# First attention by pairs of heads in a software pipeline, with value products alternating between column halves

## The reference, cut to what matters

```python
logits = jnp.einsum('bnqhgd,bnshd->bhgnqs', q, k_blk, preferred_element_type=jnp.float32) * (HEAD_DIM ** -0.5)
logits = logits + bias.reshape(N_KV_HEADS, GROUP, 1, BLOCK, 2 * BLOCK)
logits = jnp.where(valid, logits, -jnp.inf)
m = jnp.maximum(logits.max(axis=-1, keepdims=True), sink)
p = jnp.exp(logits - m)
denom = p.sum(axis=-1, keepdims=True) + jnp.exp(sink - m)
probs = (p / denom).astype(v_blk.dtype)
o = jnp.einsum('bhgnqs,bnshd->bnqhgd', probs, v_blk)
return o @ w_o + b_o
```

## Time and profile before

| | |
|---|---|
| median of 3 runs | 1185.15 us (1185.14 to 1188.02) |
| profiled execution, its own time | 1187.22 us |
| its span, first to last instruction | 1185.4 us |
| mean granted TensorE clock | 0.925 |
| TensorE busy | 1071.2 us, 90% of the span |
| first attention | 309.9 to 384.1 us |

### The profile page before, as it was taken

The page is one execution under the profiler, slowest core; times in us unless marked ns, Lnnn a source line. Parts: engine busy times, 40 slices in busy tenths (PEclk is TensorE's granted clock), DMA queues, the critical chain, the costliest instruction groups (busy, mean ns, idle before and its releaser), DMA issues.

```text
span 1185.4 us, 17311 instructions
## 1 busy us (share of the span) xinstructions
PE 1071.2 (90%) x7061; PEld 889.1 (75%) x7062; DVE 521.9 (44%) x944; ACT 404.1 (34%) x682; POOL 152.8 (13%) x216
## 2 busy tenths in 40 slices
PE   3799999989787879999996999879899999999966
PEld 2599999988755869999995999678555646646556
DVE  5545554336632255554336538674232222222254
ACT  3443333433343353334335556633201101101053
POOL 5233331110000123333011000000100000000000
PEclk8799999999766889999998999878899999999988
DMA  6334433436400115453453332048288988988501
GB/s 261 142 107 177 167 143 133 160 122 277 152 1 1 72 71 172 182 190 117 176 216 118 143 112 80 1 170 340 94 356 339 380 336 350 372 339 351 214 1 36
DMA packets 25645, 212.52 MB, mean 179 GB/s; under 512 B 2000, under 2 KB 5344, under 8 KB 5728
## 3 DMA queue, kind: packets, MB, share of 16 engines
q1 hardware_dynamic: 25568, 211.43, 46.2%
HBM read 210.35 MB, written 1.07 MB: 178 GB/s over the span
## 4 chain that ended last, share of the span: by engine, by line
PE 81%; DVE 6%; ACT 5%; issue 3%; POOL 3%; DMA 0%; POOLq 0%; DVEq 0%; ACTq 0%
PE ps L1107 45%; PE ps L1443 9%; PE ps L1428 5%; PE ps L1457 5%; PE ps L1465 4%; PE ps L1098 3%; DVE mix L1564 2%; DVE wl L613 2%; ACT wh L606 2%; POOL sq L479 1%; ACT work L752 1%; PE ps L1201 1%; PE ps L1200 1%; PE ps L1413 1%; PE ps L1144 1%
## 5 line engine op out<-in xcount | busy, mean ns | idle before, releaser
L613 DVE TENSOR_TENSOR wl<-ring,wh 128x2048 fp32r<-128x2048 f32 (+2 forms) x110 | 223.3, 2034 | 225.3 <-ACT wh L606 225.3
L606 ACT ACTIVATE wh<-ring 128x2048 fp32r<-128x2048 f32 (+2 forms) x110 | 187.1, 1705 | 318.6 <-PE ps L1107 314.1
L1107 PE MATMUL ps<-xh,wh 128*128 128x256 f32 (+3 forms) x760 | 218.9, 288 | 8.9 <-DVE xl L2074 7.0
L1107 PE MATMUL ps<-xh,wl 128*128 128x256 f32 (+3 forms) x760 | 216.6, 285 | 0.0
L1107 PE MATMUL ps<-xl,wh 128*128 128x256 f32 (+3 forms) x760 | 216.4, 285 | 0.0
L1107 PEld LDWEIGHTS ps<-xh,wh 128*128 128x128 f32 (+3 forms) x760 | 143.2, 188 | 10.9 <-issue 9.2
L1107 PEld LDWEIGHTS ps<-xh,wl 128*128 128x128 f32 (+3 forms) x760 | 143.2, 188 | 0.2
L1107 PEld LDWEIGHTS ps<-xl,wh 128*128 128x128 f32 (+3 forms) x760 | 143.1, 188 | 0.0
L1443 PE MATMUL ps<-wring,xb 128*64 128x512 f32 x512 | 112.7, 592 | 2.3 <-issue 2.3
L1107 PE MATMUL ps<-acth,wh 128*128 128x272 f32 (+1 forms) x352 | 102.6, 292 | 3.8 <-POOL actl L494 3.8
L1107 PE MATMUL ps<-acth,wl 128*128 128x272 f32 (+1 forms) x352 | 101.4, 288 | 0.0
(11 more groups left out here) (334 smaller groups left out, 1618.5 us busy)
## 6 DMA issues: line engine op xcount, KB each, us to landing
wring<-in_w_eg SPq DMA_DIRECT2D x32, 2048.0 KB, 10.4
ring<-in_w_gu SPq DMA_DIRECT2D x22, 2048.0 KB, 7.9
wring<-in_w_ed SPq DMA_DIRECT2D x16, 2048.0 KB, 8.3
ring<-in_w_dn SPq DMA_DIRECT2D x16, 1408.0 KB, 5.9
ring<-in_w_z SPq DMA_DIRECT2D x7, 2048.0 KB, 7.8
ring<-in_w_out SPq DMA_DIRECT2D x4, 1152.0 KB, 5.1
ring<-in_w_q SPq DMA_DIRECT2D x2, 2048.0 KB, 14.0
ring<-in_w_o SPq DMA_DIRECT2D x2, 2048.0 KB, 10.5
```

The costliest lines, as they stand in the source:

```text
L606: act.activation(wh[:, j, 0:size], ring[:, slot, j * size:(j + 1) * size], ACT.Copy)\
L613: dve.tensor_tensor(wl[:, j, 0:size], ring[:, slot, j * size:(j + 1) * size], wh[:, j, 0:size].bitcast(F32), ALU.subtract).then_inc(sem("l ...
L1107: ins = mm(o, p, q, start=first and n == 0, stop=last and n == 2)
```

## The change

The unit is now a pair of heads u = 0 to 7 (`HEAD_PAIRS`). Its four tiles t are ordered by block first: both heads' block 0, then both heads' block 1, one PSUM bank each. TensorE runs scores(u + 2), turn(u), outputs(u - 1); DVE runs shares(u), logits(u + 2), attended_low(u - 2); ACT runs exps(u + 1), turned(u), attended_high(u - 1). Maximum, exponentials and scalings are for four tiles at a time, so the small operations come eight times. `outputs(u)` makes each of the four steps for head 2u and then head 2u + 1, so that successive products go to the left and right column half. The last transpose turns keys 0 to 127 of block 0 in place of the 16 meta keys alone, so that ACT copies a head's 512 columns in one instruction. `pT` has four buffers. The low part of w_o's second half moves from before the first logits to after logits(1). The removed loops are those printed above; the diff shows the new code.

```diff
-        pT = [mix[:, 2 * i:2 * i + 2, :].rearrange("p a b -> p (a b)")[:, 0:4 * P] for i in range(2)]
+        pT = [mix[:, 2 * i:2 * i + 2, :].rearrange("p a b -> p (a b)")[:, 0:4 * P] for i in range(4)]
...
+        HEAD_PAIRS = NH // 2
+        def keys_of(t):
+            return (0, N_META + P) if t < 2 else (N_META, 2 * P)
+        def weights_of(u, t):
+            return lg[u % 4 // 2][:, u % 2 * 4 + t, :]
...
+            def exps(u):
+                act.wait_ge(sem("negm_ready"), u + 1)
+                for t in range(4):
+                    n, k = keys_of(t)[1], 4 * u + t
+                    v = weights_of(u, t)[:, 0:n]
                     act.activation(v, v, ACT.Exp, bias=small[:, 32 + k:33 + k], accum_out=small[:, 96 + k:97 + k])\
                        .then_inc(sem("exp_ready"), 1)
+                k = 4 * u
+                act.activation(small[:, 64 + k:68 + k], small[:, 64 + k:68 + k], ACT.Exp).then_inc(sem("exp_ready"), 1)
+            def turned(u):
+                for h in (2 * u, 2 * u + 1):
                     act.wait_ge(sem("pt_psum"), h + 1)
+                    if u >= 2:
+                        act.wait_ge(sem("o_done"), u - 1)
+                    act.activation(pT[h % 4], ps[:, 4 + h % 2, :], ACT.Copy).then_inc(sem("pt_ready"), 1)
+            def attended_high(u):
+                act.wait_ge(sem("o_done"), u + 1)
+                o = ps[:, 6 + u % 2, 0:SEQ].rearrange("p (b q) -> p b q", q=P)
+                act.activation(xh[:, u, :].rearrange("p (b q) -> p b q", q=P), o[:, :, ::-1], ACT.Copy)\
+                   .then_inc(sem("oh_ready"), 1)
+            exps(0)
+            for u in range(HEAD_PAIRS):
+                if u + 1 < HEAD_PAIRS:
+                    exps(u + 1)
+                turned(u)
+                if u:
+                    attended_high(u - 1)
+            attended_high(HEAD_PAIRS - 1)
...
+            def scores(u):
+                for t in range(4):
+                    h, b = 2 * u + t % 2, t // 2
+                    rows = slice(t % 2 * HD, t % 2 * HD + HD)
+                    first, n = keys_of(t)
+                    if u:
+                        pe.wait_ge(sem("lg_ready"), 4 * (u - 1) + t + 1)
+                    mm(ps[:, t, 0:n], qT[rows, u, b * P:(b + 1) * P], kT[rows, h // 8, first:first + n],
+                       start=True, stop=True).then_inc(sem("s_psum"), 1)
+            def turn(u):
+                for j in range(2):
+                    h = 2 * u + j
+                    pe.wait_ge(sem("p_ready"), 4 * u + 3 + j)
+                    if u:
+                        pe.wait_ge(sem("pt_ready"), h - 1)
+                    near, far = weights_of(u, j), weights_of(u, 2 + j)
+                    turned = ps[:, 4 + j, :]
+                    pe.transpose(turned[:, 0:P], near[:, N_META:N_META + P], ident)
+                    pe.transpose(turned[:, 3 * P:4 * P], near[:, 0:P], ident)
+                    pe.transpose(turned[:, P:2 * P], far[:, 0:P], ident)
+                    pe.transpose(turned[:, 2 * P:3 * P], far[:, P:2 * P], ident).then_inc(sem("pt_psum"), 1)
+            def outputs(u):
+                pe.wait_ge(sem("pt_ready"), 2 * u + 2)
+                if u >= 2:
+                    pe.wait_ge(sem("o_ready"), u - 1)
+                v = slice(u // 4 * HD, u // 4 * HD + HD)
+                steps = ((0, vtok[0:N_META, 0, v], N_META, 3), (0, vtok[:, 1, v], P, 0),
+                         (1, vtok[:, 1, v], P, 1), (1, vtok[:, 2, v], P, 2))
+                for q, (b, value, rows, at) in enumerate(steps):
+                    for j in range(2):
+                        ins = mm(ps[j * HD:j * HD + HD, 6 + u % 2, b * P:(b + 1) * P], value,
+                                 pT[(2 * u + j) % 4][0:rows, at * P:(at + 1) * P], start=(q % 2 == 0), stop=(q % 2 == 1))
+                ins.then_inc(sem("o_done"), 1)
             pe.wait_ge(sem("q_ready"), KD)
             scores(0)
+            scores(1)
+            for u in range(HEAD_PAIRS):
+                if u + 2 < HEAD_PAIRS:
+                    scores(u + 2)
+                turn(u)
+                if u:
+                    outputs(u - 1)
+            outputs(HEAD_PAIRS - 1)
...
-                   5: ("w_o", halves("w_o", 0, PIECE)[0]), 7: ("w_o", halves("w_o", 0, PIECE)[1])}
+                   5: ("w_o", halves("w_o", 0, PIECE)[0])}
...
+            def logits(u):
+                if u == 0:
                     dve.wait_ge(sem("bias_ready"), 16)
+                if u >= 4:
+                    dve.wait_ge(sem("pt_psum"), 2 * (u - 3))
+                for t in range(4):
+                    n, first = keys_of(t)[1], P - N_META if t < 2 else 0
+                    i = 4 * u + t
                     dve.wait_ge(sem("s_psum"), i + 1)
+                    dve.tensor_tensor_reduce(out=weights_of(u, t)[:, 0:n], in0=ps[:, t, 0:n],
+                                             in1=brev[:, 2 * u + t % 2, first:SEQ], scale=1.0, scalar=-3e38,
                                              op0=ALU.add, op1=ALU.max, accum_out=small[:, i:i + 1])\
                        .then_inc(sem("lg_ready"), 1)
+                k = 4 * u
+                dve.wait_ge(sem("lg_ready"), k + 4)
+                m = small[:, k:k + 4].rearrange("p (b h) -> p b h", b=NB)
+                sink = R("sinks", 2, 2 * u).unsqueeze(1).to_broadcast([P, NB, 2])
                 chain(dve.tensor_tensor(m, m, sink, ALU.max))
+                dve.tensor_tensor(small[:, 64 + k:68 + k].rearrange("p (b h) -> p b h", b=NB), sink, m, ALU.subtract)
+                dve.tensor_scalar(small[:, 32 + k:36 + k], small[:, k:k + 4], -1.0, None, ALU.mult)\
                    .then_inc(sem("negm_ready"), 1)
+            def shares(u):
+                k = 4 * u
+                dve.wait_ge(sem("exp_ready"), 5 * (u + 1))
+                den = small[:, 96 + k:100 + k]
+                chain(dve.tensor_tensor(den, den, small[:, 64 + k:68 + k], ALU.add))
+                chain(dve.reciprocal(den, den))
+                for t in range(4):
+                    v = weights_of(u, t)[:, 0:keys_of(t)[1]]
+                    dve.tensor_scalar(v, v, den[:, t:t + 1], None, ALU.mult).then_inc(sem("p_ready"), 1)
+            def attended_low(u):
+                dve.wait_ge(sem("oh_ready"), u + 1)
+                o = ps[:, 6 + u % 2, 0:SEQ].rearrange("p (b q) -> p b q", q=P)[:, :, ::-1]
+                dve.tensor_tensor(xl[:, u, :].rearrange("p (b q) -> p b q", q=P), o,
+                                  xh[:, u, :].bitcast(F32).rearrange("p (b q) -> p b q", q=P), ALU.subtract)\
+                   .then_inc(sem("o_ready"), 1)
             logits(0)
+            logits(1)
+            split_lo(dve, "w_o", *halves("w_o", 0, PIECE)[1])
+            for u in range(HEAD_PAIRS):
+                shares(u)
+                if u + 2 < HEAD_PAIRS:
+                    logits(u + 2)
+                if u >= 2:
+                    attended_low(u - 2)
+            for u in range(HEAD_PAIRS - 2, HEAD_PAIRS):
+                attended_low(u)
```

More of the change, by code:

```diff
@@ L1789, in logits @@
+                dve.tensor_scalar(small[:, 32 + k:36 + k], small[:, k:k + 4], -1.0, None, ALU.mult)\
                    .then_inc(sem("negm_ready"), 1)
-            GROUPS = NH // HEADS_PER_GROUP
-            logits(0)
-            for g in range(GROUPS):
-                if g + 1 < GROUPS:
-                    if g:
-                        dve.wait_ge(sem("pt_psum"), HEADS_PER_GROUP * g)
-                    logits(g + 1)
-                k = PER * g
-                dve.wait_ge(sem("exp_ready"), (PER + 1) * (g + 1))
-                den = small[:, 96 + k:96 + k + PER]
-                chain(dve.tensor_tensor(den, den, small[:, 64 + k:64 + k + PER], ALU.add))
-                chain(dve.reciprocal(den, den))
-                for i in range(PER):
-                    n = N_META + P if i % 2 == 0 else 2 * P
-                    v = lg[g % 2][:, i, 0:n]
-                    dve.tensor_scalar(v, v, den[:, i:i + 1], None, ALU.mult).then_inc(sem("p_ready"), 1)
-                for h in range(HEADS_PER_GROUP * g, HEADS_PER_GROUP * (g + 1)):
-                    if h % 2 == 1:
-                        c = h // 2
-                        dve.wait_ge(sem("oh_ready"), c + 1)
-                        o = ps[:, 6 + c % 2, 0:SEQ].rearrange("p (b q) -> p b q", q=P)[:, :, ::-1]
-                        dve.tensor_tensor(xl[:, c, :].rearrange("p (b q) -> p b q", q=P), o,
-                                          xh[:, c, :].bitcast(F32).rearrange("p (b q) -> p b q", q=P), ALU.subtract)\
-                           .then_inc(sem("o_ready"), 1)
```

22 lines of the change are left out of this document (removed).

## The result

The changed kernel takes 1143.66 us at the median of six runs (1142.03 to 1149.82) against 1186.33 for the kernel before in six; the ratio is 0.9634, with an interval of 0.9611 to 0.9658. It is 42.7 us faster. I forecast 1152, in a range of 1144 to 1165: the direction was right, the size was 8 us short, and the time lies just under the range. Beside the last two experiments one of the nine runs of the kernel before was a slow one of 4486.35 us; the ratios leave it out, and the median of the other eight is 1189.21.

What follows compares the result with a forecast made beforehand. First attention, 74.2 us on the chain with TensorE and softmax taking turns, was the bound. Savings of 27 us at 1.2 GHz and 39.6 at 2.4, half the work at each, gave 33: from 1185.15 to 1152 us, range 1144 to 1165.

Steps and rivals of the forecast that it cites:

- Rows of the stage, and that the whole of it lies on the path: First attention, first score product to first w_o product: 74.2 us, all on the chain that sets the end.
- The column halves run at once; a pair for one head's price: Value products on TensorE: two heads overlap, a pair costing 2.09 us at 1.2 GHz, 1.16 at 2.4.
- The start: Beginning of first attention: with w_o's split behind logits(1), the first turn comes at 317.55 us instead of 322.13.
- A step at the upper clock: One pair of heads in the stage at 2.4 GHz: 3.6 us, set by DVE with TensorE close behind.
- I take half the work at each level: Stage's clock: half the work at 1.2 GHz, half at 2.4, so it ends at 350.7, saving 33 us.
- my sum at 2.4 GHz: Whole stage at the upper clock: DVE sets it, it ends at 344.5, saving 39.6 us.
- The clock, weighed: Granted clock in the stage: rises because value products fill both column halves, falls only where TensorE waits.
- 1 (clock low throughout): Clock stays at 1.2 GHz through the stage and into w_o: saved 24 us, 1161 us; chance 0.22.
- 2 (no overlap): Column halves of value products do not overlap: 16.7 us more at the lower level, 1172 us; chance 0.08.
- 3 (lock): Each pipeline step waits for the one before: 11 us a pair, 1199 us, deciding from 9.3; chance 0.02.
- 4: Gain given back elsewhere or the stage was covered: time within 0.3%; chance 0.02.
- What the profile would show: Stage afterwards: first w_o pass at 344 to 357, no TensorE gap over 1 us after 318, DVE busy 4 us more.

Runs made afterwards that it cites:

- the last two experiments: Kernel before with every head's value products made three times, 1247.65 us (ratio 1.0444); kernel before with every head's transposes made three times, 1192.12 us (1.003).
- Pipeline alone: Changed kernel with the first head's four value products before the second's, so successive products stay in one column half: 1152.67 us, ratio 0.9687.
- alternation alone: Kernel before, with its four groups and softmax waits, where only the value products of two heads alternate between column halves: 1166.45 us, ratio 0.9826.
- transposes three times: Kernel before with every head's four transposes made three times: 1192.12 us, ratio 1.003 to the kernel before.
- the later split: Changed kernel with the low part of w_o's second half moved behind the last shares: 1143.70 us against 1143.35 unaltered.
- split first: Changed kernel with the low part of w_o's second half back ahead of the first logits: 1146.31 us, ratio 0.9638.

## Why the prediction was off, by its own steps

- **Rows of the stage, and that the whole of it lies on the path.** Right. 41.7 us less in the stage gave 42.7 in the median.
- **The column halves run at once; a pair for one head's price.** Right: 1.17 us forecast at 1.16, and 2.10 at 1.2 GHz forecast at 2.09. Pipeline alone and alternation alone take 33.0 and 17.9 us off the stage, both together 41.7: in the pipeline, which is mostly at 2.4 GHz, the alternation is worth only 8.6.
- **The start.** The first turn was forecast 7.6 us after the first score product (317.55 less 309.93) and came after 7.31.
- **A step at the upper clock.** Forecast 3.6, measured 3.09 to 3.28. DVE's term was mis-sized: 3.55 by my sum, 3.27 measured, most of it around the maximum (0.35 instead of 0.55). There the change removed one wait between two of the three operations (they start 0.08 apart and no longer 0.20), and my 0.55 held the tail of the last one. The first steps have no low part. With a fully high clock I had the stage end 34.6 us after its start; it ended after 32.5 with 3.5 us of low clock in it.
- **"I take half the work at each level".** This is the step that failed. It took 6.2 us off the gain of 39.6. Only 3.5 of 32.5 us were at 1.2 GHz. This term of 6.2 and the 2 us by which the stage beat even my sum at 2.4 GHz are the 8 us.
- **The clock, weighed.** I expected the rise because the value products fill both halves. The rise came, but that reason is wrong: head by head the clock is up as well, from 320.4 us to the end, so that I had the rise right was luck. I also misread a row: not all low stretches mix transposes and half-filled products; from 313.90 to 319.79 there are score products alone, on the filled array, and the clock stayed at 0.50. What I had right is that it falls only where TensorE waits. In the stage of every profile here it fell in a wait of 1.39 us or more or within 1.6 us behind one. Once at 2.4 GHz in the pipelined kernels, whose longest wait from there on is 1.02 us, it stayed up to the end of the stage, half-filled products or not (65.9 us). The kernel before lost it twice, at the end of the first long wait (313.9) and at 341.3, 1.6 us behind the second of its four waits for DVE's scaling; the waits between and after found it down already. So the pipeline does two things: it hides the softmax, and it takes away the waits in which the clock falls. Why the clock comes up as early as it does, 3.5 us after the first turn, is less clear. Eight transposes, four scores and eight transposes stand there, and transposes are what the runs connect with a rise; but the pipeline alone took 5.3 us from its first turn with the same instructions. Of the Trainium skill's rule in "TensorE: Matmul & The Clock Gate", on PE-mode transpose, that transposes don't count as busy, the trace here shows the opposite for this kernel's float32 transposes: sixteen in a row were followed by a rise in two groups of four (alternation alone), 24 in a row in four of four (transposes three times).
- **Rivals.** 1 (clock low throughout) did not occur: the clock read 1.00 in 29 of the 32.5 us. 2 (no overlap) would have given 8.6 us less, not 16.7, as the clock is up; the alternation alone and its removal exclude it. 3 (lock) did not occur; steps are 3.3 us against the 9.3 at which it decides. 4 did not occur.
- **What the profile would show.** DVE's busy time was to rise by 4 us and rose by 1.0; TensorE gaps were to stay under 1 us, and the largest is 1.02, for DVE's scalings (336.90). The w_o passes start at 342.80, ahead of the 344 to 357 named.

What stays open: what decides when the clock rises, as the same work left it down and lifted it (in the kernel before it rose at 334.4 after the kind of work that left it down at 351.39); and whether the later split's 1.65 us reach the total.

## What to carry to other kernels

When engines take turns at a small stage, price the stage at both clock levels, and price a pipeline with the clock up if it removes the waits in which the clock falls; half and half was a hedge and no estimate. Keep TensorE's waits short first: that is what all these profiles support. To begin a packed stretch with transposes rather than with products that fill a column half helped in some groups and not in others (alternation alone: two of four), so it is worth a trial and no more. Products of 64 output columns on the same moving length should go to the two halves by turns, for one's price.

## What the runs showed of the hardware that I had not expected

Work that holds the granted clock need not lift it soon: 65.9 us at 1.00 and 22.8 us at 0.50 were both over three quarters value products head by head. The state at the start differed most; the mix differed a little too, as the first has scores and transposes in a fifth of its time and the second transposes in a seventh. Score products over both row halves left the clock at 0.50 for 5.9 us. 128 more transposes cost 1.8 us, as the mean clock rose from 0.61 to 0.82. And a first turn 1.3 us later (split first) made the stage 2.4 us longer, in a profile whose clock was down for 10.2 us instead of 3.4.
